# Values of the second memories made inside the two memory attentions, and the S5 and delta schedule two weight slots shorter

## The reference

```python
def first_block(x, mem, ...):                       # one layer
    h = h + _mixer(_rmsnorm(h, ...), ...)           # gated delta rule | S5, then w_out
    h = h + _cross_attn(_rmsnorm(h, ...), mem, norm_mem_g, w_xq, w_xk, w_xv, w_xo)
    h = h + _swiglu(_rmsnorm(h, ...), w_gate, w_up, w_down)
    return _rmsnorm(h, norm_final_g)

def second_block(x, mem, ...):                      # layers 0 and 1
        h = h + sb_moba_mixer(hn, ...)              # layer 0; fox_mixer in layer 1
        h = h + memory_cross_attention(rmsnorm(h, norm_xa_g[layer]), rmsnorm(mem, norm_mem_g[layer]),
                                       xa_w_q[layer], xa_w_kv[layer], xa_w_out[layer])
        h = h + conv_ffn(rmsnorm(h, ...), ...)

def memory_cross_attention(h, mem_h, w_q, w_kv, w_out):
    q = (h @ w_q).reshape(B, S, XA_HEADS, XA_HEAD_DIM)          # 4 heads of 64
    kv = (mem_h @ w_kv).reshape(B, M, 2, XA_HEADS, XA_HEAD_DIM)
    k, v = kv[:, :, 0], kv[:, :, 1]
    s = jnp.einsum('bshd,bmhd->bhsm', q, k) * (XA_HEAD_DIM ** -0.5)
    p = jax.nn.softmax(s, axis=-1)
    return jnp.einsum('bhsm,bmhd->bshd', p, v).reshape(B, S, XA_DIM) @ w_out
```

## Time and profile before

| what | value |
|---|---|
| median of 3 runs | 1231.95 us (1230.72 to 1232.10) |
| the profiled execution's own time | 1230.85 us |
| its span | 1229.1 us |
| TensorE (PE) busy | 1186.0 us, 97% of the span |
| DVE, ACT, POOL busy | 812.3, 656.3, 233.2 us |
| mean granted clock of TensorE | 0.995 |
| DMA | 188.60 MB, 342 weight loads of 512 KB |
| slots in the opening's loop | 41 |

### The profile page before, as it was taken

How to read it: one execution, slowest core, us unless ns; L and a number is a source line. 1 busy time by engine, 2 the same in 40 slices (tenths; PEclk the granted TensorE clock), 3 DMA queues, 4 the chain that set the end, 5 groups by cost and what they waited for, 6 DMA issues and landing times.

```text
span 1229.1 us, 24075 instructions
## 1 busy us (share of the span) xinstructions
PE 1186.0 (97%) x9808; PEld 1112.7 (91%) x9808; DVE 812.3 (66%) x1440; ACT 656.3 (53%) x1128; POOL 233.2 (19%) x158
## 2 busy tenths in 40 slices
PE   7999999899999999999999999999999989999997
PEld 5888789899999999898888999999888868999997
DVE  4897766654644544667866767677655577777776
ACT  3346446654544444555556555555655556555554
POOL 4030000111123223021010232322212100323230
PEclk9999899999999999999999999999999999999999
DMA  8333334534565666533343565555443342655651
GB/s 328 128 122 103 120 106 143 166 104 146 186 192 182 189 176 187 154 121 121 121 138 121 155 188 185 177 189 171 159 133 117 125 137 86 190 187 174 192 178 42
DMA packets 51661, 188.60 MB, mean 153 GB/s; under 512 B 5728, under 2 KB 5856, under 8 KB 51040
## 3 DMA queue, kind: packets, MB, share of 16 engines
q1 hardware_dynamic: 51552, 187.07, 48.1%
HBM read 186.00 MB, written 1.05 MB: 152 GB/s over the span
## 4 chain that ended last, share of the span: by engine, by line
PE 80%; DVE 8%; ACT 6%; issue 4%; DMA 0%; POOL 0%; DVEq 0%; SPq 0%; ACTq 0%
PE banks L465 60%; PE banks L495 7%; ACT w_hi L1172 3%; DVE w_lo L1733 2%; PE banks L538 1%; PE banks L967 1%; DVE h L2160 1%; PE banks L523 1%; PE banks L981 1%; ACT squares L1188 1%; PE banks L586 1%; PE banks L947 1%; PE banks L884 1%; PE banks L861 1%; DMA w_raw<-in_weights 0%
## 5 line engine op out<-in xcount | busy, mean ns | idle before, releaser
L465 PE MATMUL banks<-a_hi,w_hi 128*128 128x256 f32 x1432 | 411.4, 287 | 9.2 <-DVE a_lo L1745 5.6
L1172 ACT ACTIVATE w_hi<-w_raw 128x1024 fp32r<-128x1024 f32 x313 | 328.7, 1051 | 155.6 <-PE banks L465 155.3
L465 PE MATMUL banks<-a_lo,w_hi 128*128 128x256 f32 x1432 | 405.1, 283 | 0.0
L465 PE MATMUL banks<-a_hi,w_lo 128*128 128x256 f32 x1432 | 405.0, 283 | 0.0
L2550 POOL TENSOR_TENSOR w_lo<-w_raw,w_hi 128x1024 fp32r<-128x1024 f32 x85 | 207.4, 2440 | 846.5 <-ACT w_hi L1172 846.5
L1733 DVE TENSOR_TENSOR w_lo<-w_raw,w_hi 128x1024 fp32r<-128x1024 f32 x228 | 280.0, 1229 | 84.3 <-ACT w_hi L1172 83.9
L465 PEld LDWEIGHTS banks<-a_hi,w_hi 128*128 128x128 f32 x1432 | 274.5, 192 | 13.6 <-DVE a_lo L1745 7.7
L465 PEld LDWEIGHTS banks<-a_lo,w_hi 128*128 128x128 f32 x1432 | 274.6, 192 | 0.4
L465 PEld LDWEIGHTS banks<-a_hi,w_lo 128*128 128x128 f32 x1432 | 274.5, 192 | 0.0
L465 PE MATMUL banks<-b_hi,w_hi 128*128 128x256 f32 x880 | 253.9, 289 | 10.0 <-DVE b_lo L2323 3.4
L465 PE MATMUL banks<-b_lo,w_hi 128*128 128x256 f32 x880 | 248.9, 283 | 0.0
(11 more groups left out here) (388 smaller groups left out, 1324.1 us busy)
## 6 DMA issues: line engine op xcount, KB each, us to landing
w_raw<-in_weights SPq DMA_DIRECT2D x342, 512.0 KB, 3.6
arena<-in_mem SPq DMA_DIRECT2D x2, 1024.0 KB, 8.9
h<-in_x SPq DMA_DIRECT2D x1, 1024.0 KB, 5.1
early<-in_mem SPq DMA_DIRECT2D x1, 1024.0 KB, 14.3
out_h<-h SPq DMA_DIRECT2D x4, 256.0 KB, 2.6
cons<-in_cons SPq DMA_DIRECT2D x1, 546.0 KB, 7.6
arena<-in_late SPq DMA_DIRECT2D x1, 448.0 KB, 4.2
pars<-in_pars SPq DMA_DIRECT2D x1, 290.5 KB, 3.0
```

The lines of the kernel that those rows point to most:

```text
L465: ins = mm(out, l, r, start=start and n == 0, stop=stop and n == 2, skip_group_check=check)
L1172: do(WHI[:, ring(n), :], RAW[:, n % RAW_SLOTS, :], ACT.Copy).then_inc(*inc("w_hi_made", ("w_hi", n)))
```

## The change

The two slots of `m_v0` leave the opening and take the place of `m_v1` in `xa0`; the two slots of `m_v1` go to the same place in `xa1`, which had none. The opening's loop has 39 slots. Its table is renumbered: the last five S5 rounds are one to two slots earlier (rounds from number 3 on now follow each other every two slots), and so are the output groups, the norms, the gates (one slot earlier), betas (one), delta products (two) and everything behind them (two). The roots of both memories are made at slot 19 in place of 20, and the first memory's parts from slot 20 on; silu of `z` and the sigmoid of the gates' rows are both at slot 21.

Layer 0's gained memory is needed again for `m_v0`. It is loaded a third time, into `K1`, and that load waits on SP until the last values of `ab` have been made; ACT multiplies it by the gains within the residual of `ab_o`, one tile before each `a_hi`. In both attentions the values' copy out of the accumulators (`tok_out`, L1283) now stands before the copies of turned heads 1 to 3.

```diff
-LATE_MEMORY = {"x_q": "m_k1", "m_q0": "m_v1"}
+LATE_MEMORY = {"x_q": "m_k1", "m_q0": "m_v0", "m_q1": "m_v1"}
...
-STEPS = [(name, j) for name in ("w_in", "m_k0", "m_v0", "x_v", "x_k")
+STEPS = [(name, j) for name in ("w_in", "m_k0", "x_v", "x_k")
          for j in range(SHAPE[name][0] * SHAPE[name][1] // 8)]
-ROUND_AT = (4, 7, 10, 13, 16, 18, 20, 22)
+ROUND_AT = (4, 7, 10, 12, 14, 16, 18, 20)
...
-OUT_AT = {12: 0, 18: 1, 23: 2, 27: 3}
-Y_AT = {13: 0, 19: 1, 24: 2, 28: 3}
-L2_AT = {22 + i: i for i in range(4)}
-GATES_AT, BETA_AT, KK_AT, Y0_AT = 26, 27, 28, 30
-LEVEL_AT = {31 + i: i + 1 for i in range(6)}
-VT_AT = 29
-VN0_AT, KS_AT, VN1_AT, O1_AT = 37, 38, 39, 40
+OUT_AT = {12: 0, 17: 1, 21: 2, 25: 3}
+Y_AT = {13: 0, 18: 1, 22: 2, 26: 3}
+L2_AT = {20 + i: i for i in range(4)}
+GATES_AT, BETA_AT, KK_AT, Y0_AT = 25, 26, 26, 28
+LEVEL_AT = {29 + i: i + 1 for i in range(6)}
+VT_AT = 27
+VN0_AT, KS_AT, VN1_AT, O1_AT = 35, 36, 37, 38
 MEM2A_AT = {12 + m: m for m in range(KD)}
-MEM1_AT = {22 + i: range(2 * i, 2 * i + 2) for i in range(4)}
+MEM1_AT = {20 + i: range(2 * i, 2 * i + 2) for i in range(4)}
...
+                if s == FIRST["ab_o"] + 7:
+                    sp.wait_ge(*at(("o", "ab", 7)))
+                    sp.dma_start(K1, io["mem2"]).then_inc(*inc("mem2_third", "mem2v", by=16))
...
-                if s == 20:
+                if s == 19:
                     for i, tag in enumerate(("mem2", "mem1")):
                         pe.wait_ge(*at(("ssq", tag, KD - 1)))
...
                 for h in range(4):
-                    if l == 0 and h % 2 == 0:
-                        tok_slot("m_v1", h // 2, MEM2L, late)
+                    if h % 2 == 0:
+                        memory, ready = ((K1, "mem2v"), (MEM2L, "mem2l"))[l]
+                        tok_slot(f"m_v{l}", h // 2, memory, lambda k: ("whole", ready, k))
...
-                if s == 20:
+                if s == 19:
                     ln_exp()
                     rstd("mem2", MR2, bank[5][:, 0:T])
                     rstd("mem1", MR1, bank[5][:, T:2 * T])
...
-                if s == 23:
+                if s == 21:
                     act.wait_ge(*at("ab"))
                     do(GATE[32:36, 1, :], GATE[32:36, 1, :], ACT.Sigmoid).then_inc(*inc("delta_act", "beta_rows"))
                     ln_exp()
-                if s == 24:
+                if s == 22:
                     delta_gate_rows()
-                if name == "m_v0" and j == 1:
-                    act.wait_ge(*at(("rc", "mem2")))
-                    tok_out(name, 0, VM[:, 0, :, :], 2)
...
-            def residual(name, tag, g):
+            def residual(name, tag, g, between=None):
                 K, M = SHAPE[name]
                 for m in range(KD):
                     ahead(FIRST[name] + (m * K + K - 1) // 8)
+                    if between:
+                        between(m)
                     hi_gained(tag, m, A, H[:, m, :], g, ("h", tag, m))
...
                 ahead(FIRST["m_o" + tag[2]])
+                tok_out("m_v" + tag[2], 0, VM[:, int(tag[2]), :, :], 2)
                 for h in range(1, 4):
                     memory_turned(tag, h)
-                if tag == "xa0":
-                    tok_out("m_v1", 0, VM[:, 1, :, :], 2)
...
-            residual("ab_o", "xa0", "g2_xa0")
+            residual("ab_o", "xa0", "g2_xa0", lambda m: gained("mem2v", m, K1, K1, "g2_mem0"))
```

More of the change, by code:

```diff
@@ L81, in in_turn @@
             yield from (unit(b, u) for u in range(20))
-        elif name[:3] in ("ab_", "fox") and name[-2:] != "_o" or name in ("m_k1", "m_v1"):
+        elif name[:3] in ("ab_", "fox") and name[-2:] != "_o" or name in LATE_MEMORY.values():
             continue
@@ L282, in build @@
         H = sb("h", [P, KD, T])
-        K1, V1 = sb("k1", [P, KD, T]), sb("v1", [P, TT, D])
+        K1, V1 = sb("k1", [P, KD, T])[:], sb("v1", [P, TT, D])[:]
         KM, VM = sb("k_mem2", [P, 2, 2, T]), sb("v_mem2", [P, 2, TT, T])
@@ L391, in build @@
         SBM = [area(9216 + 768 * i, 2, 384) for i in range(2)]
-        late_turned = [a[:].rearrange("p a b -> p (a b)")[:, 768 * i:768 * (i + 1)].rearrange("p (a b) -> p a b", a=2)
+        late_turned = [a.rearrange("p a b -> p (a b)")[:, 768 * i:768 * (i + 1)].rearrange("p (a b) -> p a b", a=2)
                        for a in (K1, V1) for i in range(2)]
@@ L780, in _ @@
                 x, ready = {"w_in": (XG, "x"),
-                            "m_k0": (MEM2, "mem2a"), "m_v0": (MEM2, "mem2a"), "x_v": (B, "mem1"),
+                            "m_k0": (MEM2, "mem2a"), "x_v": (B, "mem1"),
                             "x_k": (B, "mem1")}[name]
-                if s == 20:
+                if s == 19:
                     for i, tag in enumerate(("mem2", "mem1")):
@@ L826, in _ @@
                     delta_kk()
-                if s == 22:
+                if s == 20:
                     rstd_cols("mem2", MR2, bank[6])
@@ L1380, in gained @@
             def gained(tag, m, dst, src, g):
-                act.wait_ge(*at(tag if tag == "mem2l" else tag[0:4]))
+                act.wait_ge(*at(tag if tag in ("mem2l", "mem2v") else tag[0:4]))
                 do(dst[:, m, :], src[:, m, :], ACT.Copy, scale=par(g, m)).then_inc(
@@ L1448, in _ @@
                     delta_rhs()
-                if s == 33:
+                if s == 31:
                     act.wait_ge(*at(("s5_y", 3)))
                     do(YS, YS, ACT.Gelu_apprx_tanh).then_inc(*inc("delta_act", "gelu"))
-                if 36 <= s < 40:
-                    m = s - 36
-                    hi("glu", m, A, YS[:, m, :], "gelu", after=("slot", FIRST["m_v0"] + 1), key="glu_hi")
+                if 34 <= s < 38:
+                    m = s - 34
+                    hi("glu", m, A, YS[:, m, :], "gelu", after=("slot", FIRST["m_k0"] + 1), key="glu_hi")
             def glu_out(m):
@@ L2124, in _ @@
                     delta_first()
-                if 36 <= s < 40:
-                    lo("glu", s - 36, A, YS[:, s - 36, :], ("glu_hi", "glu_lo"))
+                if 34 <= s < 38:
+                    lo("glu", s - 34, A, YS[:, s - 34, :], ("glu_hi", "glu_lo"))
             for i in range(4):
```

## The result

The change takes 1248.71 us (median of 4 runs, 1247.61 to 1250.21) against 1231.34 us (median of 4, 1229.12 to 1232.10). The ratio is 1.0140, 95% interval 1.0128 to 1.0153: slower by 17.3 us. Each ratio's interval is about 1.0 to 2.0 us wide to either side, so a difference between the change and another kernel is known to some 2 to 2.5 us; what is finer than that is read from traces.

What follows compares the result with a forecast made beforehand. TensorE, 97% busy, was taken as the bound, with DVE the engine to watch in the opening. Terms -4.5 + 3.7 - 0.4 + 2.2 = +1.0 gave 1231.85 profiled, 1233.0 median; own range 1230.5 to 1235.5, with rivals 1229.3 to 1237.3.

Steps and rivals of the forecast that it cites:

- Step 1: Opening, to the inverse's second level: two slots fewer, but DVE and ACT chains hold part back; -4.5 us.
- A: Opening: time when DVE ends the argument of round 6, behind which the roots stand; 101.0 in place of 94.8.
- A+13.3: Opening: DVE finishes reading the gates' rows and columns, for which TensorE's first L2 product waits about 2 us.
- the 3.0 that I took back for the half clock: Opening, behind the wait at the gates: the 6.82 us half-clock stretch would go, returning 3.0 of up to 3.4 us.
- Rival C: Opening: half clock stays behind new waits of 1 to 2 us, 3.0 isn't given back; 1236.0 us, chance 0.08.
- signs of being wrong: Listed failures: no DVE wait for b_hi, load wait under 1 or over 6 us, 0.50 clock in the opening.
- Behind it the order is the old one: From the inverse's second level on: TensorE is bound by its own work, so the opening's -4.5 carries through.
- rival B: Opening: POOL's adds lengthen DVE's arguments, making round 6's argument end at 102, one us more; 1234.0 us, chance 0.12.
- Step 2: Residual of ab_o: ACT waits at the first gain for the third memory load, landing after 5.5 us; +3.7 us.
- Step 3: Layer 0's memory attention: the values' copy no longer stands ahead of the last parts; -0.4 us.
- Step 4: Layer 1's memory attention: two slots come in, partly hidden by the softmax wait, and the half clock goes; +2.2 us.
- A+6.1: Opening: time when ACT has made the first b_hi part, which DVE needs for b_lo ahead of scan 6.

Runs made afterwards that it cites:

- e4: The change with DVE's copy of the keys' result moved ahead of the scan of the same slot; 1242.03 us, ratio 1.0090.
- e1: The change with POOL's slot rule in the second block's mixers set to s % 3 == 1, restoring POOL's old weights; 1245.02 us, ratio 1.0107.
- e3: The change with the eight gains of the memory's third load placed behind results 2 to 7 of the ab_o residual; 1245.73 us, ratio 1.0117.
- e5: The change with DVE's b_lo parts of the first memory moved behind the scan and argument of the same slot; 1245.31 us, ratio 1.0115.
- e6: The change with both DVE edits, keys' copy ahead of the scan and b_lo behind scan and argument; 1238.76 us, ratio 1.0052.
- e2: The kernel before with only POOL's slot rule altered (s % 3 == 2), giving POOL the change's weights; 1235.51 us, ratio 1.0033.
- e10: The kernel before with DVE's b_lo parts moved behind the scan and argument of the same slot; 1231.04 us, ratio 1.0000.
- e7: The change with four edits: POOL's old weights, later gains, keys' copy ahead of the scan, b_lo behind scan and argument; 1232.49 us, ratio 1.0007.
- e11: e7 with the delta rule's products one slot later (27); 1233.93 us, ratio 1.0015.
- e12: e7 with the values' slots in both attentions ahead of heads 0 and 1 in place of 0 and 2; 1232.53 us, ratio 1.0004.
- e8: The kernel before with m_v1's slots moved to layer 1's attention, values copied ahead of turned heads 1 to 3, POOL's weights kept; 1231.33 us, ratio 0.9998.

## Why the prediction was wrong

**Step 1, the opening** (forecast -4.5, measured +4.5). Its chain held up to the first L2 product: A 100.5 for 101.0, DVE's wait 4.2, the product at 114.0 for A+13.3 = 114.3. The sentence that failed is "The next L2 product then lets `x_v` begin at A+21.2 = 122.2": it began at 127.98, 5.8 later, and the way from there to the second level took 36.9 in place of 33.7. I followed ACT, the slowest list up to there, and didn't ask what else `x_v`'s first slot needs: a free bank, which DVE frees behind scan 7. The earlier trace rows had the sign of it, the 0.40 for `v_mem` at the same place: a wait for a bank, which I booked as gone with `m_v0`, when the bank's next reader was the copy of the keys. Shown by e4, which moves the copy alone and gains 6.2, and by the start of `x_v` behind it in e1, e3 and e5. I had priced DVE's wait for `b_hi` but taken it to be paid for by ACT's later work; e5 shows 3.1 for it, 4.7 once the copy is out of the way (e6 less e4).

Also failed: the 3.0 that I took back for the half clock. Rival C had this, at 0.08 and a price of 3.0. The stretches came in four places of the opening, 17.1 us in place of 6.8. The first 6.8, ahead of `x_v`, cost nothing; the other 10.2 are 5.1 us, where the forecast had left 0.4. The half clock in the opening was named among the signs of being wrong, and it came.

**No step at all: POOL's slots** (0, measured 4.1 in e1 and e2). The prediction said "Behind it the order is the old one". I compared the order of instructions at the places that the diff names, not POOL's list in the two mixers. The Trainium skill's rule that I cited for the opening ("SBUF — State Buffer", Who interferes with whom: such a pair shuts each other out for a whole instruction) is what happens in the fox mixer, 0.42 against 2.50; I had asked about it only where the diff stood. As rival B, in the opening, it cost nothing extra, because the pairs changed: the kernel before has two of the arguments' `TENSOR_SCALAR` pairs beside POOL's adds, 1.43 long where the one at 93.44 takes 0.46. The change has none of these and three lengthened groups of convolution steps in place of two, and A came half a microsecond early. The first of them before, DVE and POOL:

```profile
70.41 1.43 DVE L1812 TENSOR_SCALAR arena<-cons,small 128x128 f32<-128x128 f32 x2
...
70.30 1.47 POOL L2560 TENSOR_TENSOR mem_squares<-mem_squares,squares 128x256 f32<-128x256 f32 x2 [3.80 <-ACT squares L1188]
```

**Step 2, the residual** (+3.7, measured +2.6): mechanism right, size 1.1 too high. Landing 4.9 for 5.5; at the second `a_hi` the delay is 3.3, and the residual then wins 0.6 back, where I had "nothing catches up". e3 gives 2.8 back.

**Step 3** (-0.4, measured 0.0). The new copy stands where the values of head 0 wait for it; TensorE waits 0.2 for `v_mem` in each layer. The prediction had only counted what no longer stood ahead of the last parts.

**Step 4** (+2.2, measured +2.7): mechanism right, the clock included, size off by the 0.4 of step 3. The 2.7 leans on a half-clock stretch that the kernel before does not always have there (4.3 without it, by e10).

**Behind the opening** (0, measured 3.1): no step of the forecast either. 1.3 of it are two stands of TensorE without a releaser and 1.5 the stretch at 251 (last section); their cause stays open.

That the forecast of 1233.0 is nearly the time of e7 is luck. e7 lacks the copy's wait and POOL's shift, which the forecast didn't know, but also the residual's delay and DVE's wait for `b_hi`, which it had counted in: `x_v` begins at 119.31 there and not at 122.2. With only the two unknown causes taken away, the change would be near 1238.4 (an estimate, 1248.7 less 6.2 and 4.1; no run has just these two), still above the range. The range left no room for that because all its widths belonged to waits I had found. A small slip: the terms of the first parts add up to A+6.3, not A+6.1; nothing hangs on it.

## What to carry to other kernels

For each place that a change makes earlier, list everything that the next matmul waits for (operands, weights, and the bank it writes), and look at what stands ahead of each of these on its own engine; the longest list up to that point isn't the next one. When a schedule takes decisions by the number of a slot, inserting or removing slots is a change of every later decision: compare every engine's list over the whole program, or tie the rule to the weight's name.

## What the runs showed of the hardware

- The granted clock is not settled by the wait in front alone. TensorE's wait of 1.49 stands at 242.4 before and at 248.6 after, followed by the same matmuls. Before, no stretch at half clock follows; after, the one at 251.19 does, with TensorE busy for all of it. e7 has it at 242.8. It costs 1.5. e1 and e3, whose code up to there is the change's, have the wait (1.49 and 1.50) and no stretch.
- Executions of one kernel differ by their granted clock. Of the 23 of the kernel before that stand beside e11, the nine up to 1231.13 have a mean granted clock of 0.995 or 0.996, the fourteen from 1231.57 to 1234.48 have 0.992 or 0.993. So one profile doesn't give a kernel's usual stretches, and a gain of 1 to 2 us read from one has to be seen in the medians.
- In all ten kernels with the new opening TensorE stands twice inside the 32x32 products of the inverse with no releaser in the profile, at the same instructions (in e1, e3 and e12 for another 0.17 at a third); in the four with the old opening (before, e2, e8, e10) it never does. In the changed kernel this is 0.36 and 0.92:

```profile
168.08 0.39 PE L704 MATMUL banks<-arena 32*32 32x32 f32 x24 [0.36 <-issue]
...
180.77 0.26 PE L683 MATMUL banks<-arena 32*32 32x32 f32 x6 [0.92 <-issue]
```

It is 0.58 and 0.70 in e7, 2.05 and 1.01 in e11. Together they cost 1.3 to 3.1. What they are was not tried.
